# Halving the moving columns in a triangular inverse by doubling, and clearing rows in the addition

## The chip, the cores and the metric

The kernel runs on one core of a Trainium2 chip. The metric is the device time of one execution in microseconds (us). TensorE does the matmuls, VectorE, ScalarE and GpSimd the elementwise work, SyncE issues the transfers.

## The reference

One decoder layer on 256 tokens of 2048 features, all in float32:

```python
h = rmsnorm(x); z = h @ W_in                      # columns go to two head groups
y_a = rmsnorm(nsa_mixer(z_nsa))                   # sparse attention, 8 heads
y_b = rwkv7_mixer(z_rwkv)                         # 16 heads of 64: the part that matters here
x += concat(y_a, y_b) @ W_out
x += memory_attention(rmsnorm(x), rmsnorm(mem))
x += hier_moe(rmsnorm(x))                         # 32 experts
out = rmsnorm(x)
```

The RWKV part is a recurrence over the 256 tokens, for each head with a 64x64 state S:

```python
sa = S @ (-kk_t)
S = S * w_t + outer(sa, kk_t * a_t) + outer(v_t, k_t)
y_t = S @ r_t
```

The kernel does it in chunks of 64 tokens. Within a chunk the corrections `sa` of the tokens depend on each other through a strictly triangular 64x64 matrix A, so the kernel needs the inverse of (I - A) for each chunk and head.

## The kernel before

All engines have a program of their own, written out in order, and they meet by semaphores that count steps (`Progress`: `mark` counts one up, `at` gives the value to wait for). TensorE's order is fixed by hand. The large projection (`w_in`) is cut into small steps of three matmuls (`product`, lines 783 and 788) and these fill the gaps: each call `gap()` issues as many of them as the list `GAPS` says. So where TensorE would wait for another engine in the RWKV part, it does filler products instead.

The RWKV heads are done in four groups (`for g in range(NGRP)`), four heads each, as two pairs (`pi`) whose heads lie on partitions 0 to 63 and 64 to 127 (`HEADS`). With four chunks of 64 tokens a group has 16 triangular matrices of 64x64: 8 column blocks `k` (4 in each of two token tiles `tt`) on 2 row blocks `r`. They lie in tiles of 128x512.

The inverse is made by doubling, in `for lv in LV` (levels 1 to 5). Before level lv the diagonal blocks of size b = 2^lv are inverted already; after level 5 the whole matrix is. `X[:, 0]` holds the inverse in one orientation and `X[:, 1]` its transpose. `AM` is A masked to the off-diagonal blocks that the level joins (`MTk[:, lv]` is the mask, made once by GpSimd). A level does, on full 64x64 blocks:

1. TensorE, line 906: P = AM^T X0, 16 calls into bank 2. Each call is two records in the trace, the two passes of an fp32 matmul. Weights are 64x64, 64 columns move.
2. three filler products; meanwhile ScalarE, line 1513, copies P (128x512) to `Ps`, and GpSimd, line 2525, masks the next level's AM once P has been done.
3. TensorE, line 916 (not at level 5): new parts of X0, into bank 5; then line 921: new parts of X1, into bank 7. 16 calls each.
4. VectorE, line 2010: adds bank 5 to X0, then bank 7 to X1, 128x512 each. P of the next level waits for the first, line 921's of the next level for the second.

After level 1 and 2 TensorE also does transposes (lines 932 and 941). After level 5 the chunk recurrence starts (lines 956 and 959) and needs X1. Line 837 (head sums, two moving columns), 845, 881 and 892 are other fp32 products of a group, line 1023 belongs to the sparse attention; all serve as comparison below.

Of the kernel before, what the change touches and what calls it, by code (L numbers as in the profile page):

```python
# [23 lines left out]
ALU = mybir.AluOpType  # L24
ACT = mybir.ActivationFunctionType
AX = mybir.AxisListType
# [48 lines left out]
def decoder_layer(nc, x_in, mem, ln1_g, w_in, cmp_pos_k, cmp_w1_k, cmp_w2_k, cmp_pos_v, cmp_w1_v,  # L75
# [5 lines left out]
    with ctx:  # L81
# [54 lines left out]
        start = FIXED  # L136
# [3 lines left out]
        r1 = Region(start, ARENA)  # L140
# [6 lines left out]
        M2, MTk, M0 = masks[:, 0:2], masks[:, 2:8], masks[:, 8]  # L147
# [22 lines left out]
        X = r1.take(2, 2, 4, CH)  # L170
        AM = flat_view(tH, 2, 4, CH)
# [2 lines left out]
        Zs = r1.take(2, CH)  # L174
        Us = r1.take(2, CH)
        small_k, small_v = r1.take(8), r1.take(8)
        HI = 47744
        assert r1.at <= HI
        piece_at = [2 * UN, 2 * UN + 2 * PW, 3 * UN, 3 * UN + 2 * PW, HI + 8 * T, HI - 2 * PW - 384]
# [140 lines left out]
        def b2(i, n=2):  # L320
            return bank[i][:, :].rearrange("p (a b) -> p a b", a=n)
# [266 lines left out]
        def by_partition(ap):  # L588
            return ap.rearrange("q (p c) -> q c p", c=NC)

        def bc(ap, *shape):
            return ap.broadcast_to([ap.shape[0], *shape])

# [155 lines left out]
        def _(pe):  # L749
# [98 lines left out]
            for g in range(NGRP):  # L848
# [45 lines left out]
                mm.then_inc(*pe_rw.mark(("AK", g)))  # L894
                gap()

                for lv in LV:
                    if lv == 1:
                        pe.wait_ge(*dve_rw.at(("G", g, 1)))
                        pe.wait_ge(*pool_rw.at(("AM", g, 1, 1)))  # L900
                    else:
                        pe.wait_ge(*pool_rw.at(("AM", g, lv)))
                        pe.wait_ge(*dve_rw.at(("X", g, lv - 1, 0)))
                    for k in range(8):
                        for r in HEADS:
                            mm = pe.matmul(b2(2, 8)[r, k, :], AM[r, k // 4, k % 4, :], X[r, 0, k // 4, k % 4, :],  # L906
                                           start=True, stop=True)
                    mm.then_inc(*pe_rw.mark(("P", g, lv)))
                    gap()
                    pe.wait_ge(*act_rw.at(("Ps", g, lv)))  # L910
                    if lv > 1:
                        pe.wait_ge(*dve_rw.at(("X", g, lv - 1, 1)))
                    if lv < 5:
                        for k in range(8):
                            for r in HEADS:
                                mm = pe.matmul(b2(5, 8)[r, k, :], X[r, 1, k // 4, k % 4, :], Ps[r, k // 4, k % 4, :],  # L916
                                               start=True, stop=True)
                        mm.then_inc(*pe_rw.mark(("X", g, lv, 0)))
                    for k in range(8):
                        for r in HEADS:  # L920
                            mm = pe.matmul(b2(7, 8)[r, k, :], Ps[r, k // 4, k % 4, :], X[r, 1, k // 4, k % 4, :],  # L921
                                           start=True, stop=True)
                    mm.then_inc(*pe_rw.mark(("X", g, lv, 1)))
                    gap()
                    if lv == 1:
                        pe.wait_ge(*dve_rw.at(("AK", g)))
                        for tt in range(NT):
                            for k, c, pi in pairs(tt):
                                for j in range(2):
                                    for r in HEADS:  # L930
                                        at = (2 * k + j) * CH
                                        mm = pe.matmul(bank[3 + 3 * tt][r, at:at + CH], BK[r, j, pi, chunk(c)],
                                                       ident[r, r], start=True, stop=True)
                        mm.then_inc(*pe_rw.mark(("trb", g)))
                    if lv == 2:
                        pe.wait_ge(*act_rw.at(("trb", g)))
                        for c in range(NCH):
                            for pi in range(2):
                                for r in HEADS:
                                    at = (2 * c + pi) * CH  # L940
                                    mm = pe.matmul(bank[3][r, at:at + CH], z[r, 4 + pi, chunk(c)], ident[r, r],
                                               start=True, stop=True)
                        mm.then_inc(*pe_rw.mark(("trv", g)))
# [441 lines left out]
        def _(act):  # L1385
# [102 lines left out]
            for g in range(NGRP):  # L1488
                act.wait_ge(*dve_rw.at(("ssm", g)))
                A(small_k, small_k, ACT.Sqrt).then_inc(*act_rw.mark(("sq1", g)))  # L1490
                act.wait_ge(*pe_rw.at(("wa", g)))
                if g:
                    act.wait_ge(*dve_rw.at(("out", g - 1)))
                for pi in range(2):
                    cw, ca = 2 * g + pi, 8 + 2 * g + pi
                    A(tA[:, pi, :], b2(2)[:, pi, :], ACT.Tanh, bias=prm2[:, cw:cw + 1], scale=0.5)
                    ins = A(tB[:, pi, :], b2(3)[:, pi, :], ACT.Tanh, bias=prm2[:, ca:ca + 1], scale=0.5)
                ins.then_inc(*act_rw.mark(("th", g)))
                gap()

                act.wait_ge(*dve_rw.at(("D", g)))
                A(flat(tE), flat(tD), ACT.Exp, scale=-KAPPA)
                A(flat(tH), flat(tD), ACT.Exp, scale=KAPPA)
                A(flat(tA), flat(tA), ACT.Exp, scale=-KAPPA)
                A(em, tC.rearrange("p a (c t) -> p a c t", t=CH)[:, :, :, CH // 2 - 1], ACT.Exp, scale=-KAPPA)\
                    .then_inc(*act_rw.mark(("exp", g)))
                ready(ACT.Sqrt, 4 + g)
                gap()
                gap()
                gap()  # L1510
                for lv in LV:
                    act.wait_ge(*pe_rw.at(("P", g, lv)))
                    nc.scalar.copy(Ps.rearrange("p a b c -> p (a b c)"), bank[2][:, :])\
                        .then_inc(*act_rw.mark(("Ps", g, lv)))
                    gap()
                    if lv == 1:
                        act.wait_ge(*pe_rw.at(("trb", g)))
                        for tt in range(NT):
                            ins = nc.scalar.copy(BKt[:, 2 * tt:2 * tt + 2].rearrange("p a b c d -> p (a b c d)"),
                                                 bank[3 + 3 * tt][:, :])  # L1520
                        ins.then_inc(*act_rw.mark(("trb", g)))
                    if lv == 2:
                        act.wait_ge(*pe_rw.at(("trv", g)))
                        nc.scalar.copy(Vt.rearrange("p a b c -> p (a b c)"), bank[3][:, :])\
                            .then_inc(*act_rw.mark(("trv", g)))
                    gap()
                for c in range(NCH):
                    act.wait_ge(*pe_rw.at(("Z", g, c)))
                    nc.scalar.copy(flat(Zs), bank[2][:, 0:P]).then_inc(*act_rw.mark(("Zs", g, c)))
                    gap()  # L1530
                    gap()
                    if c < NCH - 1:
                        gap()
                act.wait_ge(*pe_rw.at(("Y", g, NCH - 1)))
                nc.scalar.copy(flat(tA), bank[7][:, :]).then_inc(*act_rw.mark(("ys", g)))
                gap()
                gap()
                act.wait_ge(*dve_rw.at(("ve", g)))
                A(small_v, small_v, ACT.Sqrt).then_inc(*act_rw.mark(("sq2", g)))
                gap()  # L1540
                gap()
# [290 lines left out]
        def _(dve):  # L1832
# [90 lines left out]
            dve.wait_ge(*pe_c.at("gates"))  # L1923
            V.tensor_scalar(gates, b2(3, 16)[:, 0:2, 0:24], 0.5, 0.5, ALU.mult, ALU.add).then_inc(*dve_c.mark("gates"))
            dve.wait_ge(*pool_c.at("masks"))

            for g in range(NGRP):
                def mix(j):
# [70 lines left out]
                for lv in LV:  # L1999
                    gap()  # L2000
                    for i in range(2):
                        if lv == 5 and i == 0:
                            continue
                        dve.wait_ge(*pe_rw.at(("X", g, lv, i)))
                        if lv > 1:
                            dve.wait_ge(*dve_rw.at(("X", g, lv - 1, i)))
                        elif i:
                            dve.wait_ge(*pool_rw.at(("X0", g, 1)))
                        o = X[:, i].rearrange("p a b c -> p (a b c)")
                        V.tensor_tensor(o, o, bank[5 + 2 * i][:, :], ALU.add).then_inc(*dve_rw.mark(("X", g, lv, i)))  # L2010
                    gap()
                for c in range(NCH):
                    gap()
# [597 lines left out]
```

## Time and profile before

| | us |
|---|---|
| median of 3 runs | 1705.63 (1703.72 to 1706.48) |
| profiled execution, its own time | 1708.4 |
| its span | 1706.4 |
| TensorE busy in the span | 1619.1 (95%) |
| VectorE busy | 1092.5 (64%) |
| ScalarE busy | 858.7 (50%) |
| GpSimd busy | 80.8 (5%) |

The span is the time from the first to the last instruction; the execution's own time has a little around it. The granted TensorE clock over the whole span was 0.98. In the RWKV part it stood at 1.00 except in four places: after the wait at level 1 of group 0 (110 to 112 us: 0.50) and of group 2 (302 to 304: 0.50), after a wait for a weight transfer (370 to 378: 0.50), and near the end of group 3 (458 to 464: 0.50). A row of a group gives line, engine, operation, what is written and read, the shape, the count, busy time and the mean duration of one. In a matmul row "64*64 64x64" means weights with 64 rows and 64 columns, and a moving operand of 64 rows and 64 columns. `PE` is a matmul, `PEld` a weight load. Durations of matmuls overlap, so the pitch (start to start) is less than the duration of one.

### The profile page before, as it was taken

To read this page: it belongs to the slowest core of one execution; us is meant where nothing else is said; L and a number is where in the kernel's file an instruction comes from. 1 tells how busy PE (TensorE), PEld (TensorE's weight loads), DVE (VectorE), ACT (ScalarE), POOL (GpSimd) and SP (SyncE) were. 2 spreads that over 40 slices of the span, in tenths; PEclk is the share of its full clock that TensorE was granted. 3 is DMA by queue.
4 is the path that set the end of the run, shared out by engine and by line. 5 is a ranking of instruction groups with operands and counts; after the bars stand their busy time and mean duration, and the time that the engine had idled before them with its cause. 6 is when DMAs were issued, how large, how long until landed. Compare 5 with 4: busy or idle time off the path is not lost.

```text
span 1706.4 us, 29604 instructions
## 1 busy us (share of the span) xinstructions
PE 1619.1 (95%) x12494; PEld 1428.9 (84%) x12494; DVE 1092.5 (64%) x1370; ACT 858.7 (50%) x1063; POOL 80.8 (5%) x136
## 2 busy tenths in 40 slices
PE   6999999989989999999999999889999999999996
PEld 6998989879888899998899988678877887887884
DVE  4664838355345455445453344588889889889896
ACT  5532424233245444454453343457776776776774
POOL 5020101102100000000000000000000000000000
PEclk9999999989999999999999999899999999999998
DMA  6541506042283443437536163279999978998993
GB/s 212 158 146 35 171 2 200 7 155 80 76 278 118 149 130 120 146 106 270 190 125 197 50 195 109 99 296 374 370 353 343 381 295 316 378 376 337 368 375 139
DMA packets 155321, 350.92 MB, mean 206 GB/s; under 512 B 12912, under 2 KB 110794, under 8 KB 129738
## 3 DMA queue, kind: packets, MB, share of 16 engines
q1 hardware_dynamic: 155210, 349.30, 57.5%
q8 instruction: 87, 1.43, 0.3%
q14 instruction: 24, 0.20, 0.0%
HBM read 347.18 MB, written 2.10 MB: 205 GB/s over the span
## 4 chain that ended last, share of the span: by engine, by line
PE 80%; DVE 12%; DMA 2%; ACT 2%; POOL 1%; issue 1%; SPq 1%; DVEq 0%; ACTq 0%
PE bank L788 18%; PE bank L1302 18%; PE bank L1131 10%; PE bank L1321 9%; PE bank L1151 5%; PE bank L783 4%; DVE split L2235 3%; DVE piece L1880 2%; PE bank L808 1%; PE bank L906 1%; PE bank L921 1%; DMA compress_v_weights<-in_cmp_w_v_dram 1%; PE bank L916 1%; PE bank L1265 1%; DVE arena_phases L2339 1%
## 5 line engine op out<-in xcount | busy, mean ns | idle before, releaser
L2235 DVE TENSOR_TENSOR split<-weights_raw,split 128x2048 fp32r<-128x2048 f32 x192 | 438.4, 2290 | 56.2 <-ACT split L1731 52.9
L1731 ACT CAST split<-weights_raw 128x2048 fp32r<-128x2048 f32 x192 | 366.9, 1913 | 97.1 <-PE bank L1302 48.4
L1302 PE MATMUL bank<-split,gathered_hi 128*128 128x512 f32 x1024 | 321.6, 395 | 7.1 <-DVE split L2235 7.1
L788 PE MATMUL bank<-hidden_lo_chunks,piece 128*128 128x256 f32 x928 | 266.1, 287 | 0.0
L1461 ACT CAST piece<-arena_fixed 128x1024 fp32r<-128x1024 f32 (+1 forms) x160 | 163.7, 1035 | 200.8 <-PE bank L788 137.3
L1880 DVE TENSOR_TENSOR piece<-arena_fixed,piece 128x1024 fp32r<-128x1024 f32 (+1 forms) x160 | 192.5, 1223 | 89.7 <-ACT piece L1461 89.1
L1302 PEld LDWEIGHTS bank<-split,gathered_hi 128*128 128x128 f32 x1024 | 190.5, 189 | 48.7 <-DVE split L2235 10.0
L1302 PE MATMUL bank<-split,gathered_lo 128*128 128x512 f32 x512 | 200.9, 392 | 0.0
L788 PE MATMUL bank<-hidden_hi_low_chunks,piece 128*128 128x256 f32 x928 | 182.1, 294 | 4.5 <-DVE hidden_lo_chunks L1866 4.5
L788 PE MATMUL bank<-hidden_hi_high_chunks,piece 128*128 128x256 f32 x928 | 183.4, 296 | 0.0
L788 PEld LDWEIGHTS bank<-hidden_lo_chunks,piece 128*128 128x128 f32 x928 | 181.6, 196 | 0.0
L2133 DVE TENSOR_TENSOR loop_split<-arena_fixed,loop_split 128x2048 fp32r<-128x2048 f32 x48 | 107.9, 2288 | 111.7 <-ACT loop_split L1627 111.7
L1321 PE MATMUL bank<-split,hidden_hi 128*128 128x512 f32 x512 | 161.1, 395 | 1.4 <-DVE hidden_lo L2377 1.0
L788 PEld LDWEIGHTS bank<-hidden_hi_low_chunks,piece 128*128 128x128 f32 x928 | 146.8, 195 | 11.5 <-DVE hidden_lo_chunks L1866 4.7
L788 PEld LDWEIGHTS bank<-hidden_hi_high_chunks,piece 128*128 128x128 f32 x928 | 148.4, 197 | 6.9 <-issue 4.1
L1627 ACT CAST loop_split<-arena_fixed 128x2048 fp32r<-128x2048 f32 x48 | 89.7, 1925 | 88.6 <-PE bank L1131 65.5
L1131 PE MATMUL bank<-loop_split,act_over_concat 128*128 128x512 f32 x384 | 128.9, 390 | 0.0
L1321 PEld LDWEIGHTS bank<-split,hidden_hi 128*128 128x128 f32 x512 | 95.8, 187 | 25.3 <-issue 1.2
L1302 PEld LDWEIGHTS bank<-split,gathered_lo 128*128 128x128 f32 x512 | 96.7, 189 | 21.1
L1321 PE MATMUL bank<-split,hidden_lo 128*128 128x512 f32 x256 | 101.0, 395 | 0.0
L1151 PE MATMUL bank<-act_over_concat,loop_split 128*128 128x256 f32 x512 | 92.3, 283 | 0.0
L783 PE MATMUL bank<-piece,hidden_lo_chunks 128*128 128x256 f32 x320 | 90.4, 283 | 0.0
(381 smaller groups left out, 2310.4 us busy)
## 6 DMA issues: line engine op xcount, KB each, us to landing
weights_raw<-in_moe_w_gate_dram SPq DMA_DIRECT2D x64, 1024.0 KB, 5.1
weights_raw<-in_moe_w_up_dram SPq DMA_DIRECT2D x64, 1024.0 KB, 7.2
weights_raw<-in_moe_w_down_dram SPq DMA_DIRECT2D x32, 2048.0 KB, 7.6
arena_fixed<-in_w_in_dram SPq DMA_DIRECT2D x23, 2048.0 KB, 8.9
arena_fixed<-in_wk_mem_dram SPq DMA_DIRECT2D x8, 2048.0 KB, 8.3
arena_fixed<-in_wv_mem_dram SPq DMA_DIRECT2D x8, 2048.0 KB, 8.3
arena_fixed<-in_w_out_dram SPq DMA_DIRECT2D x8, 2048.0 KB, 7.8
arena_fixed<-in_wq_mem_dram SPq DMA_DIRECT2D x8, 2048.0 KB, 8.1
```

Source lines behind the costliest of these rows:

```text
L783: mm = pe.matmul(b[:, half * UC:half * UC + UC], hidden_x(x_, c)[:, half * P:half * P + P], w(w_)[:, k % 4, :], start=False, stop=r == 2 * ...
L788: mm = pe.matmul(b[:, half * T:half * T + T], w(w_)[:, k % 8, :], hidden_x(x_, c), start=c + t == 0, stop=c == NC - 1 and t == 2)
L1131: mm = pe.matmul(b, src(x_, cc)[:, half * P:half * P + P], lspl[2 * s + h][:, y_, c * WC:c * WC + WC], start=s + h + c + k == 0, stop=end)
L1151: mm = pe.matmul(b, lspl[2 * s + h][:, y_, at:at + P], src(x_, NC // 2 * h + c), start=h + c + k == 0, stop=h == 1 and c == NC // 2 - 1 an ...
L1302: mm = pe.matmul(bank[parity][:, :], hs[a][:, group % 2, NC // 4 * off + c, :], sl[:, b, c * 2 * FF:(c + 1) * 2 * FF], start=off + c + k == 0,
L1321: mm = pe.matmul(bank[4 + q][:, :], tTs[a][:, f, :], sl[:, b, q * 512:q * 512 + 512], start=start and f + k == 0, stop=stop and f + k == 3)
L1461: nc.scalar.copy(piece_half(p, 0), raw_piece(p)).then_inc(piece_hi, 1)
L1627: nc.scalar.copy(lspl[2 * s + h][:, 0, :], slot(s)[:, h * HU:h * HU + HU]).then_inc(loop_hi, 1)
L1731: nc.scalar.copy(split_half(i, 0, j), raw_half(j, hf, tail)).then_inc(act_hi, 1)
L1880: V.tensor_tensor(piece_half(p, 1), raw_piece(p), piece_half(p, 0).bitcast(F32), ALU.subtract)\
L2133: V.tensor_tensor(sl[:, 1, :], slot(s)[:, r:r + HU], sl[:, 0, :].bitcast(F32), ALU.subtract)\
L2235: V.tensor_tensor(split_half(i, 1, j), raw_half(j, hf, tail), split_half(i, 0, j).bitcast(F32), ALU.subtract).then_inc(dve_lo, 1)
```

## The change

A level joins blocks of size b in pairs. The inverse changes only in one off-diagonal block of each pair, so in each block of 2b columns only b columns of X0 and X1 get something new. The changed kernel moves these 32 of 64 columns and writes them side by side into the first 256 columns of the bank.

```diff
+        first_rows = r1.take(6)
...
+        def halves(ap, lv, h):
+
+            return ap.rearrange("p (n h b) -> p n h b", h=2, b=1 << lv)[:, :, h, :]
+
+        def all_blocks(tile):
+            return tile.rearrange("p a b c -> p (a b c)")
...
+                def compact(b, r, k, lv):
+                    return bank[b][r, k * 32:k * 32 + 32].rearrange("p (n b) -> p n b", b=1 << lv)
+
...
-                            mm = pe.matmul(b2(2, 8)[r, k, :], AM[r, k // 4, k % 4, :], X[r, 0, k // 4, k % 4, :],
-                                           start=True, stop=True)
+                            mm = pe.matmul(compact(2, r, k, lv), AM[r, k // 4, k % 4, :],
+                                           halves(X[r, 0, k // 4, k % 4, :], lv, 0), start=True, stop=True)
...
-                                mm = pe.matmul(b2(5, 8)[r, k, :], X[r, 1, k // 4, k % 4, :], Ps[r, k // 4, k % 4, :],
-                                               start=True, stop=True)
+                                mm = pe.matmul(compact(5, r, k, lv), X[r, 1, k // 4, k % 4, :],
+                                               halves(Ps[r, k // 4, k % 4, :], lv, 0), start=True, stop=True)
...
-                            mm = pe.matmul(b2(7, 8)[r, k, :], Ps[r, k // 4, k % 4, :], X[r, 1, k // 4, k % 4, :],
-                                           start=True, stop=True)
+                            mm = pe.matmul(compact(7, r, k, lv), Ps[r, k // 4, k % 4, :],
+                                           halves(X[r, 1, k // 4, k % 4, :], lv, 1), start=True, stop=True)
...
-                    nc.scalar.copy(Ps.rearrange("p a b c -> p (a b c)"), bank[2][:, :])\
+                    nc.scalar.copy(all_blocks(Ps).rearrange("p (n h b) -> p n h b", h=2, b=1 << lv),
+                                   bc(bank[2][:, 0:256].rearrange("p (n b) -> p n b", b=1 << lv).unsqueeze(2),
+                                      256 >> lv, 2, 1 << lv))\
...
+            link(V.tensor_reduce(first_rows, MTk, AX.X, ALU.max))
...
-                        o = X[:, i].rearrange("p a b c -> p (a b c)")
-                        V.tensor_tensor(o, o, bank[5 + 2 * i][:, :], ALU.add).then_inc(*dve_rw.mark(("X", g, lv, i)))
+                        o = halves(all_blocks(X[:, i]), lv, i)
+                        new = bank[5 + 2 * i][:, 0:256].rearrange("p (n b) -> p n b", b=1 << lv)
+                        if i:
+                            ins = V.scalar_tensor_tensor(out=o, in0=new, scalar=first_rows[:, lv:lv + 1], in1=o,
+                                                         op0=ALU.mult, op1=ALU.add)
+                        else:
+                            ins = V.tensor_tensor(o, o, new, ALU.add)
+                        ins.then_inc(*dve_rw.mark(("X", g, lv, i)))
```

P's 256 new columns are written twice into `Ps` by ScalarE, into both halves of each block, since `Ps` is also used as weights, whose 64 columns stay. This doubling puts values into rows of line 921's product that must not change; VectorE's addition to X1 multiplies them by `first_rows`, which is 1 on the rows that a level may change and 0 elsewhere (a column per level, made once from the masks). The weights of all three products, the number of calls, the filler products and the waits are as before.

## Rows read from the trace of the kernel before

**Rows 1.** The page's chain that ended last, share of the span by engine

```profile
PE 80%; DVE 12%; DMA 2%; ACT 2%; POOL 1%; issue 1%; SPq 1%; DVEq 0%; ACTq 0%
```

**Rows 2.** The waits of TensorE, 90 to 480 us: total us, times, longest us

```profile
PE bank L906 <- POOL arena_phases L2525: 6.9, 4, 1.7
...
PE bank L959 <- DVE arena_phases L2010: 3.2, 4, 0.8
```

**Rows 3.** The three products of a level by line: durations in ns min/median/max, count by shape

```profile
L906 PE MATMUL bank<-arena_phases x640: 217/218/267, 108.5 to 425.4; 64*64 64x64 f32 x160
...
L916 PE MATMUL bank<-arena_phases x512: 217/218/366, 111.7 to 423.4; 64*64 64x64 f32 x171
...
L921 PE MATMUL bank<-arena_phases x640: 217/218/311, 113.3 to 427.7; 64*64 64x64 f32 x160
```

**Rows 4.** Timeline, levels 4 and 5 of group 1: start us, length us, what

```profile
222.81 1.01 PEld L916 LDWEIGHTS bank<-arena_phases 64*64 64x64 f32 x32
...
223.74 1.02 PEld L921 LDWEIGHTS bank<-arena_phases 64*64 64x64 f32 x32
...
224.01 0.69 DVE L2010 TENSOR_TENSOR arena_phases<-arena_phases,bank 128x512 f32<-128x512 f32 x1 [2.75 <-PE bank L916]
...
224.81 1.04 PEld L906 LDWEIGHTS bank<-arena_phases 64*64 64x64 f32 x32
...
225.92 0.30 PEld L788 LDWEIGHTS bank<-hidden_hi_high_chunks,piece 128*128 128x128 f32 x2
...
226.03 0.59 ACT L1513 COPY arena_phases<-bank 128x512 f32<-128x512 f32 x1 [2.77 <-PE bank L906]
...
227.18 1.01 PEld L921 LDWEIGHTS bank<-arena_phases 64*64 64x64 f32 x32
...
229.12 0.31 PEld L959 LDWEIGHTS bank<-arena_phases 64*64 64x64 f32 x8 [0.93 <-DVE arena_phases L2010]
```

**Rows 5.** Timeline, batches of fp32 matmuls with other widths and column counts

```profile
78.70 0.98 PEld L837 LDWEIGHTS bank<-arena_fixed,arena_phases 128*128 128x128 f32 x8
...
86.73 0.97 PEld L845 LDWEIGHTS bank<-arena_fixed,arena_phases 128*128 128x128 f32 x8 [0.16 <-DVE arena_phases L1948]
...
198.90 1.92 PE L892 MATMUL bank<-arena_phases 64*64 64x128 f32 x32
...
503.49 1.95 PE L1023 MATMUL bank<-arena_phases,compress_blocks 128*32 128x128 f32 x64 [2.17 <-DMA arena_phases<-in_cmp_w_k_dram]
```

**Rows 6.** Weight loads 64 and 128 columns wide, and a matmul that moves 128 columns

```profile
L906 PEld LDWEIGHTS bank<-arena_phases x640: 129/135/135, 108.5 to 425.3; 64*64 64x64 f32 x160
...
L845 PEld LDWEIGHTS bank<-arena_fixed,arena_phases x64: 186/192/333, 86.7 to 464.3; 128*128 128x128 f32 x64
...
L881 PE MATMUL bank<-arena_phases x128: 267/267/321, 100.2 to 398.3; 64*64 64x128 f32 x128
```

**Rows 7.** Groups of VectorE by line and form: busy us, mean ns | idle before

```profile
L2010 DVE TENSOR_TENSOR arena_phases<-arena_phases,bank 128x512 f32<-128x512 f32 x36 | 24.8, 688 | 65.2 <-PE bank L916 52.5 <-PE bank L921 12.8
...
L1991 DVE TENSOR_TENSOR arena_phases<-bank,arena_phases 128x256 f32<-128x256 f32 x8 | 3.3, 414 | 0.0
...
L2355 DVE SCALAR_TENSOR_TENSOR gathered_lo<-bank,arena_phases,gathered_hi 128x256 fp32r<-128x256 f32 x32 | 14.0, 479 | 4.8 <-ACT gathered_hi L1716 4.1
```

**Rows 8.** Chain of waits by time, level 1 of groups 1 and 2: start, length, what

```profile
205.67 1.26 PE bank L788 x9
...
206.93 1.08 PE bank L916 x32
...
300.51 1.82 PE bank L788 x9
...
302.34 1.90 PE bank L916 x32
```

**Rows 9.** Level 1 of groups 0 and 2: TensorE busy (count), granted clock, DMA, GB/s

```profile
110.00:112.00 2.00, 2.00 (x15) 0.50 0.00 0
...
302.00:304.00 2.00, 2.00 (x34) 0.50 0.00 0
```

## The prediction

> **What bounds the kernel now.** I began with the chain of waits on the page: TensorE carries 80% of the span, VectorE 12% [rows 1]. So time can be won only where a TensorE stretch on the chain gets shorter, or where TensorE stands still. Then the list of waits for the stretch from 90 to 480 us, the four RWKV groups, in which all of the changed code runs. TensorE waits there for the changed code's neighbours twice a group: at level 1 for GpSimd (6.9 us in 4 waits), and after level 5 for VectorE's addition (3.2 us in 4 waits) [rows 2]. In all other places of the inverse TensorE has work in hand: the timeline of one group shows product, filler matmuls and product back to back [rows 4]. The third view is the three product lines themselves: 640, 512 and 640 records, 1792 together, that is 56 batches of 32 (16 calls of two fp32 passes each), moving 64 columns against weights of 64 columns [rows 3]. The change halves the columns that move. What it is worth hangs on one question: is a record's place in the stream set by its moving columns, or by its weights?
>
> **The pitch of a batch.** The weights of line 916 begin at 222.81, those of line 921 at 223.74 [rows 4]: 0.93 us for 32 records, 29.1 ns each. The two heads of a pair lie on different rows and columns of the array and alternate, so one head's half of the array starts a record every 58 ns.
> Is that the columns? Two batches with 128x128 weights answer. Line 845 moves 128 columns, line 837 moves 2. Eight weight loads take 0.97 and 0.98 us; less one load of 0.192 us, over 7, that is 111 and 113 ns a record [rows 5, 6]. Sixty-four times fewer columns and not one ns less: below some count the weight load sets the pitch, 112 ns for 128 columns of fp32 weights. For 64 columns half of it is 56 ns a head, 28 ns a record when two heads alternate; the measured 29.1 is that already. The durations of single loads agree that width is what is paid for: 135 ns at 64 columns, 192 at 128, 0.89 ns a column [rows 6], or 57 ns for 64. Against it stands line 892, with the same 64x64 weights and 128 moving columns: (1.92 - 0.267) / 31 = 53.3 ns a record [rows 5, 6]. So columns do count above 64, and half of 53.3 is 26.7, close to 29.1: at 64 columns the two limits lie side by side. Below, only one of them falls, and the change does not touch the weights (all 64 wide).
> Bounds for the term: 0 at one end; at the other the pitch falls in proportion to the columns, 14.5 ns x 1792 = 26 us. I take 0, because the row with 2 moving columns is the only one that has few columns, and it shows nothing gained; up to 1.1 ns x 1792 = 2.0 us (down to 28.0 ns) stay inside the forecast's own range. Could it be slower? The moving operand is now read in runs of 2 to 32 elements. No row moves such runs; if it halved the reading speed, 32 columns would stream as 64 do now, which fits the present pitch. So 0 there.
> The Trainium skill (TensorE: Matmul & The Clock Gate, "Wait — 56ns, not 53.3ns?") says that the start-to-start time of matmuls never falls below about 25 ns, however few columns. By that rule alone the saving would be 4.1 ns x 1792 = 7.3 us instead of 0. The same page of the Trainium skill, under "LDWEIGHTS (loading the stationary operand)", prices a load at its columns over 1.2, which is 53 ns for 64 columns and 27 a record with two heads, 4.3 us at the most. The rows with 2 and 128 columns side with the second.
>
> **What else of the change lies on the path.**
> - After level 5 TensorE has nothing until line 2010 has added: its loads stood 0.93 us [rows 4], four times [rows 2]. The addition of 128x512 takes 0.688 us. The new one has 256 elements, a per-partition scalar and one operand in a bank; the nearest row is line 2355, 0.479 us. The same size without such a scalar is 0.414 [rows 7]. 4 x (0.688 - 0.479) = 0.8 us; bounds 0 (short runs might cost as much as they save) and 1.1. I take 0.8.
> - At levels 4 and 5 the P product follows the two X products at once, and waits for the first addition: X's second batch begins at 223.74, P at 224.81, 1.07 us later instead of 0.93; VectorE was busy from 224.01 to 224.70 [rows 4]. That is 0.14 us in 8 places. The new addition (a plain one, 0.414) ends 0.27 us earlier, and the wait is gone: 1.1 us. Bounds 0 and 1.1. What is late next is the array itself, as in the unhindered batches.
> - A batch ends in the drain of its last matmul. From P's first load to that of the filler it is 1.11 us, not 0.93 [rows 4]. A record with 128 moving columns lasts 267 ns, one with 64 lasts 218 [rows 3, 6]: 0.77 ns a column, 25 ns for 32. Twenty changes from P to filler and four waits at level 5 give 24 x 0.025 = 0.6 us; bounds 0 and, if both passes of the last pair count, 1.2.
> - Sum: 0.8 + 1.1 + 0.6 = 2.5 us saved.
>
> **What is priced at nothing, and its cover.** ScalarE's copy still writes 512 elements; only its reading repeats. It ran from 226.03 to 226.62, and TensorE asked for it at 227.18 [rows 4], with nine filler matmuls between: 0.56 us of cover. Were it twice as long (0.59 more), 20 copies would cost 0.03 each, 0.6 us. VectorE's other savings (16 x 0.27 and 16 x 0.21, some 7.7 us) are busy time that TensorE doesn't wait for. The one new reduction, 384 elements, costs between 0.414 and 0.688 by line 1991's and line 2010's sizes [rows 7] and stands on VectorE ahead of group 0; queued behind it is the mixing that leads to the head sums of line 837, and TensorE comes to these only at 78.70, straight from filler products, without a wait [rows 5]. These products cover it; without them it costs its 0.5 us once. GpSimd's wait at level 1 (1.7 us a group) has causes ahead of the changed code and stays. No DMA, no semaphore and no queue position changes.
>
> The profiled execution took 1708.4 us with a span of 1706.4, 2.8 us above the median of 1705.63. Against it the sum gives 1705.9; against the median 1703.1.
>
> **Rivals.**
> - Columns do count a little: the loads of the two heads overlap by more than half widths suggest, and the issue of records is what is left. The smallest pitch in these rows is line 1023's, (1.95 - 0.27) / 63 = 26.6 ns, with 32-column weights [rows 5]. If 64-column weights reach it, 2.5 ns x 1792 = 4.5 us more are saved: 1698.6. For it: 29.1 may hold some overhead of streaming; against: lines 837 and 845. Chance 0.15. (By the floor that the Trainium skill states this case would end at 25 ns, an estimate of 7.3 + 2.5 us saved, 1695.8; no row is as low.)
> - The product streams in proportion: 26 us, less the P product now waiting for the first addition (X's second batch 0.47 us, but 0.2 + 0.41 + 0.11 from the first's last record to P; 0.25 x 16 = 4) plus 2.0 for the rest: near 1681.5. Chance 0.05.
> - TensorE's clock, the slower side. After the 1.7 us wait at level 1 the clock fell in groups 0 and 2 (granted 0.50, the 1.2 GHz level [rows 9]) and not in groups 1 and 3. The filler then took 1.82 instead of 1.26 us and the next product 1.90 instead of 1.08 [rows 8], 1.4 us a fall. If the pitch stays while half as many columns move, the array does less in the same time, exactly there. Falls in groups 1 and 3 too cost 2.8: 1705.9, chance 0.07. If besides each fall lasts through further products and a filler (0.93 + 1.27 at half speed cost 2.2 more, four times: 8.8), the sum is 2.8 + 8.8 - 2.5 = 9.1 us slower: 1714.7; half of that lengthening gives 1710.3, which I take for this rival. It decides once falls cost over 2.5 us more than now. For it: the two falls show the margin is thin. Against: in groups 1 and 3 the same wait cost no clock, and even after a fall the clock came back within a few microseconds, during these same products. Chance 0.13.
> - The saving isn't what it says: runs of 2 elements make VectorE's half additions as long as whole ones. Then only the drain's 0.6 stays: 1705.0, inside the forecast's case.
>
> **How the numbers follow.** The forecast, 1703.1, has 0.60, with its own range 1700.8 to 1705.3. A run of this kernel tells a difference of about 0.2%, 3.4 us, from none. Of the 0.60, the part with the pitch at 28 ns and all terms at their upper bound passes 3.4: 0.18 faster, 0.40 same, 0.02 slower. With the two quicker rivals' 0.15 + 0.05 faster is 0.38; same is 0.40 + 0.07 = 0.47; slower 0.02 + 0.13 = 0.15. The range, 1696.0 to 1709.0, holds the first quicker rival with some 1.4 ns a record below its row's pitch, and the milder part of the slow one; it leaves out the proportional case (0.05) and most of the slow rival (about 0.10).
>
> **What would show it.** Records of lines 906, 916 and 921 read 64x32; a batch's loads still start 0.93 us before the next batch's (right), or 0.85 (the first rival), or about 0.5 (the second). P of levels 4 and 5 follows the second X batch in 0.93. The wait of line 959 reads about 0.72 us for its loads. VectorE's two forms read 0.41 and 0.48. The granted clock of the windows at level 1 is 0.50 in two groups; in four, or longer, the clock rival holds. My sum is wrong if the pitch moves at all, since 1 ns of it is worth 1.8 us.

## The result, and the profile after

The changed kernel took 1710.99 us (median of 20 runs, 1704.57 to 1725.5), the kernel before 1705.62 (20 runs, 1699.73 to 1707.35). The ratio is 1.004, with a 95% interval of 1.0026 to 1.0055: 4 to 9 us slower, where I had forecast 2.5 us faster. The spread grew, from 8 us to 21, all of it upwards.

The profiled execution was one of the quickest of the changed kernel: 1705.44 us, span 1703.5. Set against the one profile before (1708.4 us) it would have looked like a gain. What it shows of pitch and waits is as forecast. The three product lines (durations in ns, min/median/max; two of the three lines):

```profile
L917 PE MATMUL bank<-arena_phases x640: 192/219/292, 109.2 to 427.0; 64*64 64x32 f32 x160
...
L932 PE MATMUL bank<-arena_phases x640: 219/219/291, 112.5 to 429.3; 64*64 64x32 f32 x160
```

They answer to [rows 3]: 32 columns instead of 64. The timeline of levels 4 and 5 of group 1 answers to [rows 4]:

```profile
225.21 1.01 PEld L927 LDWEIGHTS bank<-arena_phases 64*64 64x64 f32 x32
...
226.14 1.02 PEld L932 LDWEIGHTS bank<-arena_phases 64*64 64x64 f32 x32
...
226.38 0.42 DVE L2029 TENSOR_TENSOR arena_phases<-arena_phases,bank 128x256 f32<-128x256 f32 x1 [2.77 <-PE bank L927]
...
227.07 1.02 PEld L917 LDWEIGHTS bank<-arena_phases 64*64 64x64 f32 x32
...
228.13 0.30 PEld L796 LDWEIGHTS bank<-hidden_hi_high_chunks,piece 128*128 128x128 f32 x2
...
228.25 0.59 ACT L1524 COPY arena_phases<-bank 128x512 f32<-128x512 f32 x1 [2.60 <-PE bank L917]
...
229.40 1.01 PEld L932 LDWEIGHTS bank<-arena_phases 64*64 64x64 f32 x32
...
231.10 0.31 PEld L970 LDWEIGHTS bank<-arena_phases 64*64 64x64 f32 x8 [0.70 <-DVE arena_phases L2026]
```

From 225.21 to 226.14 is 0.93 us for 32 records, to the hundredth what it was with 64 columns. P follows the second X batch after 0.93 us (227.07 - 226.14), not 1.07. From P to the filler it is 1.06 us, not 1.11. The loads of the chunk recurrence stand 0.70 us, not 0.93. ScalarE's copy is as long as it was. So each saving that I had named is there. Two groups whose clock stayed at full speed give their sum. From P of level 1 to the recurrence:

```profile
404.49 1.15 PE L906 MATMUL bank<-arena_phases 64*64 64x64 f32 x32 [1.73 <-POOL arena_phases L2525]
...
428.73 0.45 PE L959 MATMUL bank<-arena_phases 64*64 64x64 f32 x8 [0.79 <-DVE arena_phases L2010]
```

that is group 3 of the kernel before, 24.24 us, and group 3 of the changed one:

```profile
406.56 1.12 PE L917 MATMUL bank<-arena_phases 64*64 64x32 f32 x32 [1.73 <-POOL arena_phases L2545]
...
430.12 0.45 PE L970 MATMUL bank<-arena_phases 64*64 64x64 f32 x8 [0.59 <-DVE arena_phases L2026]
```

23.56 us. The difference, 0.68 us, is 2.7 us over four groups, if the others are alike.

What ate it is in the clock. Group 1 kept its clock in the kernel before (205.67 and 206.93 in [rows 8]). In the changed kernel, same stretch (busy us of PE, PEld, DVE, ACT, POOL, then the granted clock, DMA share, GB/s):

```profile
202.00:204.00 2.00, 1.02 (x32) 1.04 (x32) 1.92 (x2) 0.00 (x0) 0.83 (x1) 1.00 0.00 0
204.00:206.00 2.00, 2.00 (x13) 1.97 (x9) 0.00 (x0) 0.81 (x2) 1.09 (x1) 0.50 0.47 111
...
212.00:214.00 2.00, 2.00 (x44) 2.00 (x41) 0.00 (x0) 0.61 (x2) 0.00 (x0) 0.50 0.02 7
214.00:216.00 2.00, 2.00 (x33) 1.83 (x31) 0.00 (x0) 1.06 (x2) 1.09 (x1) 0.94 0.00 0
```

and its chain of waits in order of time (start, length, what):

```profile
202.98 1.12 PE bank L917 x32
204.10 2.22 PE bank L796 x9
206.32 1.85 PE bank L927 x32
208.17 1.71 PE bank L932 x32
209.88 3.47 PE bank L943 x64
213.35 1.37 PE bank L917 x32
214.72 1.26 PE bank L796 x9
```

The clock went to 0.50, its 1.2 GHz level, by the time of the fillers after P, and stayed there for 10 us, through both X products and the transposes (line 943). In group 2 it fell too (windows from 302 to 310 us: 0.75, 0.50, 0.50, 0.54); groups 0 and 3 kept their clock. P to the recurrence took 28.13 us in group 1 (202.98 to 231.11), 4.6 us more than in group 3. The falls of the kernel before cost 1.4 us each [rows 8]. Over the 20 runs the time and the mean granted clock of a run lie on a line, 1.5 us for each 0.001 of the clock (correlation -0.98): a run at 0.981 took 1704.57, one at 0.967 took 1725.5. The profile came from the quick end, at 0.98.

### The profile page after: what moved, and what is told of

Read it like the earlier page. It is cut to its first block, busy times and chain, and to the rows that moved or that the text cites. A ratio compares the mean times of both kernels' runs of the same rounds, so it can differ in the third digit from the quotient of the medians.

```text
span 1703.5 us, 29605 instructions
## 1 busy us (share of the span) xinstructions
PE 1620.1 (95%) x12494; PEld 1433.2 (84%) x12494; DVE 1084.2 (64%) x1371; ACT 858.5 (50%) x1063; POOL 76.3 (4%) x136
## 4 chain that ended last, share of the span: by engine, by line
PE 81%; DVE 12%; ACT 2%; DMA 2%; POOL 1%; issue 1%; SPq 1%; DVEq 0%; ACTq 0%
PE bank L1313 18%; PE bank L796 18%; PE bank L1142 10%; PE bank L1332 9%; PE bank L1162 5%; PE bank L791 4%; DVE split L2255 3%; DVE piece L1893 1%; PE bank L816 1%; PE bank L932 1%; PE bank L917 1%; DMA compress_v_weights<-in_cmp_w_v_dram 1%; PE bank L927 1%; DVE arena_phases L2359 1%; PE bank L1276 1%
```

## The experiments

Medians; before is each time the kernel before on the same chip. A clock is the median over a kernel's runs. Some kernels have times in two bunches: of the 20 runs of the kernel before above, five took 1699.7 to 1700.6 us and thirteen 1705.1 to 1707.4; of e2's twelve, seven took 1697.8 to 1700.2 and five 1703.4 to 1706.6. A median can jump by some us there, so where it matters differences are given by the ratio too; an interval of a difference of two ratios is my estimate from theirs.

| kernel | runs | us | ratio to before (95%) | clock |
|---|---|---|---|---|
| before | 15 to 25 | 1705.3 to 1706.1 | | 0.982 to 0.983 |
| e1: changed, again | 7 | 1711.49 | 1.0036 (1.0023 to 1.0050) | 0.977 |
| e2: all move 64 columns | 12 | 1699.85 | 0.9977 (0.9962 to 0.9992) | 0.984 |
| e3: level 1 moves 64 | 12 | 1700.86 | 0.9976 (0.9965 to 0.9987) | 0.984 |
| e7: only level 1 moves 32 | 10 | 1712.58 | 1.0035 (1.0023 to 1.0047) | 0.976 |
| e8: only P of level 1 moves 32 | 11 | 1703.55 | 0.9989 (0.9979 to 1.0000) | 0.982 |
| e9: only X of level 1 moves 32 | 11 | 1703.15 | 0.9997 (0.9980 to 1.0015) | 0.983 |
| e4: changed, fillers ahead of level 1 | 7 | 1695.42 | 0.9945 (0.9925 to 0.9965) | 0.985 |
| e5: e2, fillers ahead of level 1 | 5 | 1695.97 | 0.9929 (0.9915 to 0.9944) | 0.984 |
| e6: before, fillers ahead of level 1 | 5 | 1697.55 | 0.9956 (0.9942 to 0.9969) | 0.984 |

**e1, the changed kernel again.** 

> The changed kernel once more, on the chip of the next three kernels. Clock theory: the pitch of a batch is still 29 ns, TensorE's waits are about 2 us shorter than before, and yet the time is 2 to 9 us above the kernel before, because the granted clock falls more often or longer in the levels; the slower a run, the lower its mean clock. Rival (phase): the change only moves later work in time, and the extra falls come in places outside the levels. The profile shows where the 0.50 stretches are: theory, over 5 us of lost time between the starts of levels 1 and 5 of the four groups (before: 3.4); rival, no more than before there.

The loss came again on another set of runs. This profile (1708.29 us) has the long fall in group 1 once more, and further ones at level 1 of groups 2 and 3, the last of which the first profile had not. Its windows in group 3 (PE busy, count, granted clock, DMA share, GB/s):

```profile
410.00:412.00 2.00, 2.00 (x42) 0.50 0.00 0
412.00:414.00 2.00, 2.00 (x42) 0.50 0.00 0
414.00:416.00 2.00, 2.00 (x55) 0.68 0.03 8
```

Let a window of 2 us at a granted clock c count 2 x (1 - c) us as lost. In the level stretches that gives 12.0 us (5.1, 3.4 and 3.4) here, 8.5 (5.1 and 3.4) in the changed kernel's first profile, and 3.4 (two falls of 1.7) in the kernel before. The phase rival, in which the extra falls come in other places, fails: outside the levels this profile lost 27.1 us and the one before 31.4. That is also part of why these two profiles took the same time, 1708.3 and 1708.4 us.

**e2, 64 columns moved again, all else as changed.**

```diff
+        def WIDE(lv):
+            return True
+
+        def new_part(b, lv, h):
+            if WIDE(lv):
+                return halves(bank[b][:, :], lv, h)
...
+                def moved(ap, lv, h):
+                    return ap if WIDE(lv) else halves(ap, lv, h)
...
+                    if WIDE(lv):
+                        return b2(b, 8)[r, k, :]
...
-                                           halves(X[r, 0, k // 4, k % 4, :], lv, 0), start=True, stop=True)
+                                           moved(X[r, 0, k // 4, k % 4, :], lv, 0), start=True, stop=True)
...
-                        new = bank[5 + 2 * i][:, 0:256].rearrange("p (n b) -> p n b", b=1 << lv)
+                        new = new_part(5 + 2 * i, lv, i)
```

The other two products and ScalarE's copy are edited in the same way.

> As the changed kernel, with its half additions, row clearing and doubled copy, but each product moves all 64 columns again, as before the change. Clock theory: the columns that move are what the clock lost by, so this is faster than the changed kernel by 4 to 9 us, and 1 to 3 us faster than the kernel before (about 1703.5), since the shorter additions stay. Rival (phase, or something in ScalarE's or VectorE's new forms): the same as the changed kernel, about 1711.

1699.85 us: 11.6 below the changed kernel (10.1 by the ratios), more than the 4 to 9 expected. The half additions, the row clearing and the doubled copy stay in and do no harm. The edit gives back two things at once: the number of columns, and the way in which they are read. Sixty-four lie in one run, while 32 are read in runs of b, 2 elements at level 1. No run here parts the two; "32 columns" below means both together. The gain on the kernel before is 3.9 us by the ratio (1.4 to 6.5), which holds the 2.7 us of the rows. By the medians it is 6.2, since e2's median lies in its lower bunch and that of the kernel before in its upper one.

Its profile has three falls at level 1, in groups 0, 1 and 3, each of 1.7 us lost. The one in group 3, where the first window of e1's fall was followed by three more:

```profile
404.00:406.00 2.00, 2.00 (x21) 0.50 0.00 0
406.00:408.00 2.00, 2.00 (x54) 0.68 0.00 0
```

**e3, only level 1 wide; e7, only level 1 narrow.** The edit is e2's, with `lv == 1` and `lv > 1` as its condition.

> As the changed kernel, but level 1, which follows the 1.7 us wait for GpSimd, moves all 64 columns; levels 2 to 5 move 32. Clock theory as I put it in the prediction (the falls belong to the stretch right after that wait): most of the loss is gone, 1703 to 1706. Clock theory in a wider form (any level with few moving columns can let the clock fall or keep it low): 1707 to 1710. Phase rival: 1711 as the changed kernel.

> As the changed kernel, but only level 1 moves 32 columns; levels 2 to 5 move all 64. Clock theory, now put as: the products right after the wait for GpSimd decide both whether the clock falls and how long it stays down. Then level 1 alone brings the whole loss back: 1707 to 1712, although 44 of 56 batches are wide again. If few columns in levels 2 to 5 keep a fallen clock down (a rival inside the theory, which the kernel with a wide level 1 could not test, as its clock did not fall there): falls as often as in the changed kernel but shorter, 1702 to 1706.

With level 1 wide nothing of the loss is left, though 44 of 56 batches move 32 columns: 1700.86 us is e2's time, and lower than either form of the theory had said. With only level 1 narrow, 12 batches of 56, all of it is back (1712.58 us, 0.6 above the range). In levels 2 to 5, where no such wait stands ahead, few columns cost nothing that these runs can tell. Group 2 of e7, chain of waits in order of time:

```profile
302.58 1.12 PE bank L930 x32
303.70 2.17 PE bank L804 x9
305.87 1.85 PE bank L940 x32
307.72 1.71 PE bank L945 x32
309.43 3.47 PE bank L956 x64
312.89 1.47 PE bank L930 x32
314.36 1.27 PE bank L804 x9
```

Levels 2 to 5 are wide here, and the fall is as long as in group 1 of the changed kernel: it ends at the same place, at P of level 2. So few columns in the later levels aren't needed for a long fall. The profile has three falls at level 1 (5.1, 5.1 and 3.4 us lost).

**e8 and e9, part of level 1 narrow.** Against e7's condition; `b` is the bank (2 for P, 5 and 7 for X).

```diff
-        def WIDE(lv):
-            return lv > 1
+        def WIDE(lv, b):
+            return lv > 1 or b > 2
```

is e8, where only P of level 1 moves 32 columns (4 of the 56 batches), and

```diff
+            return lv > 1 or b == 2
```

is e9, where only the two X products of level 1 do (8 of the 56).

> As the changed kernel, but only the very first product of each group, P of level 1, moves 32 columns; the other 55 of 56 kinds of batches move 64. It stands between the 1.7 us wait and the fillers. Theory A (P's few columns beside the idle time let the clock fall): falls in three or four groups, each of the short kind (1.7 us of loss as in the kernel before): 1702 to 1705. Theory B (the columns moved by the two X products of level 1, after the fillers, keep the clock down): as with 64 columns everywhere, 1699 to 1701. With level 1 all narrow at 1711, the rest between would be theory B's.

> As the changed kernel, but only the two X products of level 1, which come after the first filler products, move 32 columns; its P moves 64, and so do levels 2 to 5. With only P narrow the kernel took 1703.55, with both narrow 1712.58, with neither 1699.85. Theory B alone (few columns in X keep a fallen clock down, P plays no part in that): falls come as rarely as with 64 columns everywhere but last 7 to 10 us when they come: 1703 to 1707. If trigger and length multiply (P narrow makes them frequent, X narrow makes them long), P and X each alone cost less than half of the 12.7 us that both cost: 1702 to 1706, and the profile shows at most two falls, long ones. If X narrow alone already brings the whole loss, 1709 to 1713, P's columns don't matter.

Against e2, P alone costs 3.7 us by the medians, X alone 3.3, both 12.7. By the ratios it is 2.0 (-1.1 to 5.2), 3.4 (-0.5 to 7.3) and 9.9 (6.6 to 13.2), so neither alone is clear of noise. The steps from one to both are: narrow X on top of a narrow P costs 7.8 us (5.1 to 10.6), narrow P on top of a narrow X 6.5 (2.9 to 10.1). So both take part, and "theory B alone", whose range for e9 (1703 to 1707) holds the 1703.15, fails by the second step. Whether together they cost more than the sum of the two, as "multiply" says, isn't shown: 9.9 against 5.4, and the 4.5 between is uncertain by 4.8.

What the profiles show is the length. e8, group 2 (X wide):

```profile
301.47 1.64 PE bank L804 x9
303.11 1.90 PE bank L940 x32
305.01 1.22 PE bank L945 x32
306.24 1.87 PE bank L956 x64
```

and e9, group 1 (P wide, X narrow):

```profile
207.57 1.74 PE bank L804 x9
209.31 1.85 PE bank L940 x32
211.16 1.71 PE bank L945 x32
212.87 2.89 PE bank L956 x64
```

With 64 columns in X the clock is back before the second X product ends (1.22 against 0.93 at full speed; the transposes take their usual 1.87). With 32 it isn't (1.71 and 2.89). Over all profiles: the seven falls at level 1 with 64 columns in X (two in the kernel before, three in e2, two in e8) each lost 1.7 us; the nine with 32 (two and three in the changed kernel, three in e7, one in e9) lost 3.4 or 5.1. How often the clock falls can't be read from single profiles: e2's has three falls at level 1 and e3's, with the same level 1, none. With P wide it fell in 6 of 16 places (before, e2, e3, e9), with P narrow in 10 of 16. That P's columns make falls more frequent is argued from that and from the 6.5 us above, not shown.

**e4, e5 and e6, TensorE kept at work during the wait.**

```diff
-        GAPS = [32] * FIRST + ([16, 22, 10, 5] + [3, 0] * 5 + [3] * 12 + [4, 5, 24]) * NGRP + [30]
+        GAPS = [32] * FIRST + ([16, 22, 10, 10] + [3, 0] * 5 + [3, 2] * 5 + [3] * 2 + [4, 5, 24]) * NGRP + [30]
```

> As the changed kernel, but five more filler products (15 matmuls, some 1.8 us) stand ahead of level 1, taken from five of the twelve gaps of the chunk recurrence, so that TensorE works while GpSimd masks. Clock theory: the wait at level 1 goes from 1.7 us to nothing in all four groups (6.9 us saved) and with it the idle time that lets the clock fall there: 1696 to 1702. If falls come from the few columns alone, without the idle time: 1703 to 1706. If the filler products are missed where they were taken, TensorE waits for ScalarE or VectorE in the chunks and the gain is under 3 us: 1708 or more.

> The half additions with all 64 columns moved, and the five filler products ahead of level 1. If both gains add up (no wait of 1.7 us, 6.9 us; no clock lost in the levels): 1692 to 1695, up to 3 us below the kernel with fillers and 32 columns (1695.4). If the fillers alone already keep the clock up, the few columns then cost nothing: 1695 to 1696, the same as that one.

> The kernel before with nothing changed but the place of five filler products (ahead of level 1, from the chunks' gaps). It tells what the fillers are worth by themselves: 6.9 us of waiting and the short falls at level 1, 1.7 us in about half of the groups: 1695 to 1698. The half additions are the only difference to the kernel above, so 1.9 us (4 x 0.2 and 8 x 0.14) should lie between the two.

Five filler products moved ahead of level 1 take the wait away. The two longest in total of TensorE's waits from 90 to 480 us in e4, against [rows 2]:

```profile
PE bank L845 <- DVE arena_phases L1954: 5.5, 1, 5.5
PE bank L970 <- DVE arena_phases L2026: 2.4, 4, 0.6
```

The first stands outside the levels and has 5.2 us in the kernel before. Line 917 no longer waits for GpSimd, and group 1 of e4 runs through with 32 columns at full clock:

```profile
202.14 1.05 PE bank L917 x32
203.19 1.27 PE bank L796 x9
204.46 1.05 PE bank L927 x32
205.51 0.93 PE bank L932 x32
206.44 1.89 PE bank L943 x64
208.34 0.91 PE bank L917 x32
```

In the profiles of e4, e5 and e6 no window of a level reads a granted clock below 0.97. Taking the idle time away is worth 16.1 us on the changed kernel (1711.49 to 1695.42; 15.5 by the ratios), 8.3 on the kernel before (7.5) and 3.9 on e2 (8.2). The 3.9 is less than the 6.9 us of waiting because e2's median lies in its lower bunch; by the means of the runs (1701.5 and 1694.6) it is 6.9. e4 came in 0.6 us below its expectation, e6 inside it, and e5 where it was to come if the fillers alone keep the clock up. Once the idle time is gone, 32 columns and 64 can't be told apart (1695.42 and 1695.97; 7 and 5 runs). So the long falls take both, the idle 1.7 us and the few columns after it; the idle time alone leaves the short ones of the kernel before and e2. e4 and e5 beat both kernels, by 0.55% and 0.71% of the kernel before; of e6's 8.3 us the wait itself is 6.9 [rows 2]. The 1.9 us between e5 and e6 read 1.6 by the medians and 4.6 by the ratios, with five runs each.

## Why the prediction was wrong, step by step

- The pitch. Right: 29.1 ns with 64 columns, 29.1 with 32. The two rivals in which columns count (0.15 and 0.05) are out. That it is the weight load that sets the pitch is still argued, from the rows with 128-column weights (111 and 113 ns); no run here changes the width of the weights. (Line 1023's pitch is 26.7 ns, not 26.6.) The Trainium skill (TensorE: Matmul & The Clock Gate, "Wait — 56ns, not 53.3ns?") gives a floor near 25 ns for few columns. This trace stays above it, at 29.1, and so agrees, but the floor isn't what binds. The price of a load of 64 columns in the Trainium skill (same page, "LDWEIGHTS (loading the stationary operand)"), halved for two heads (an estimate of 27), is nearer.
- The wait after level 5. Forecast 0.8 us, measured 4 x (0.93 - 0.70) = 0.9. The additions took 0.485 and 0.423 us in the mean, forecast 0.479 and 0.414.
- P of levels 4 and 5. Forecast 8 x 0.14 = 1.1, measured the same: 0.14 at the place shown, and in group 3 at both levels.
- The drain. Forecast 0.025 us a change from P to the filler. It is 0.05 at the one shown (1.11 to 1.06) and 0.04 in the mean of group 3's five, 0.8 us over twenty.
- The sum. Forecast 2.5 us, measured 4 x 0.68 = 2.7; the terms add up to it (0.23, 0.28 and 0.20 us in group 3). The reduction took 0.54 us ahead of group 0 and cost nothing that shows; ScalarE's copy was hidden as said.
- The clock. This is the step that failed: the forecast put the change of the clock at nothing, and its rival, "TensorE's clock, the slower side", had 0.13 at 1710.3. What came is 1710.99. In e1's profile the low clock lost 12.0 us in the levels instead of 3.4; 8.6 more, less the 2.7 saved, is 5.9 us slower, and the medians are 5.4 apart. The rival had the place (level 1, after the 1.7 us wait) and the lengthening right. Its price is partly luck: it put a fall in each of four groups at half of the lengthening, while the profiles have two or three longer ones. I argued it away with two rows of the kernel before: groups 1 and 3 kept their clock through the same wait, and a fallen clock "came back within a few microseconds, during these same products". They were not the same products. Those that brought the clock back moved 64 columns, and that was the very thing to be halved; e8 and e9 show that it matters. And where the clock falls in two groups of four under equal conditions, I should have taken the stretch to stand at an edge, so that a small change for the worse could move it far. Those two falls spoke for the rival. The range ended at 1709, 2 us short.
- Reading one execution as the case was the second slip: the kernel's falls differ from run to run, and so a 2.5 us sum was set against a term that varies by more (the kernel before spans 7.6 us over its 20 runs).

## What to carry to other kernels

Where every small matmul has weights of its own, halving the moving columns may buy nothing (here 29.1 ns a record with 64 as with 32, weights of 64 columns on two halves of the array), but it does take work out of the array, and right after an idle stretch of 1.7 us, at four places, that cost some 10 us (e7 against e2, by the ratios). Before making such a stretch lighter, fill the idle time ahead of it: here that alone, 8.3 us, was worth more than the 2.7 us that the change could have given. When a profile shows the clock falling at some of several equal places, treat it as a cost that moves with the change, and look at the mean clock of all runs, not at one trace.

## What the runs showed of the hardware that I had not expected

- An engine that the trace calls busy, record after record with no gap, stayed at 1.2 GHz for 10 us, through two products that moved 32 columns per record and the transposes behind them (group 1 of the changed kernel). Where these two products moved 64, it was back at 2.4 GHz during the second (e8).
- At the 1.2 GHz level a batch with 32 columns took 1.85 us, line 927 of the changed kernel, where 64 columns took 1.90, line 916 [rows 8]. A single weight load took 223 ns there in both (median), against 135 at full clock. So few columns hardly help at the low clock either.
- Filled with other matmuls, the 1.7 us ahead of level 1 left no fall at level 1 in three profiles (e4, e5, e6), with 32 columns or 64.
